# Attention by token tile instead of by head, with the output projection, norm and router of one tile between the attention items of the next

## The reference

```
h = rmsnorm(x);  z = h @ w_in                       # q, k, v and a short gated convolution
s = q.k * scale + bias[bucket];  p = softmax(s)     # 8 maps of 64, in 4 pairs ("heads")
a = p[map 0] - lam * p[map 1];   o = a @ v          # one attention item = one head, 128 queries
o = rmsnorm(o) * 0.8
x = x + concat([o, conv]) @ w_out                   # output projection
h2 = rmsnorm(x);  logits = h2 @ w_router            # one group of 4, 2 of its 4 experts
x = x + sum over chosen experts of gate * (silu(h2 Wg) * (h2 Wu)) Wd
x = x + sigmoid(x @ w_ple_gate) * rmsnorm(p @ w_ple)
```

## Time and profile before

| | |
|---|---|
| median of 3 runs | 717.28 us (713.4 to 717.65) |
| the profiled execution | 716.85 us, span 715.0 us |
| PE busy | 640.3 us, 90% |
| DVE / ACT / POOL busy | 402.9 / 331.8 / 91.1 us |
| transfers | 111 MB, mean 155 GB/s |
| TensorE clock granted, mean | 0.957 |

### The profile page before, as it was taken

How to read it: one execution, slowest core, us unless ns; L and a number is a source line. 1 busy time by engine, 2 the same in 40 slices (tenths; PEclk the granted TensorE clock), 3 DMA queues, 4 the chain that set the end, 5 groups by cost and what they waited for, 6 DMA issues and landing times.

```text
span 715.0 us, 8295 instructions
## 1 busy us (share of the span) xinstructions
PE 640.3 (90%) x3026; PEld 511.9 (72%) x3026; DVE 402.9 (56%) x675; ACT 331.8 (46%) x606; POOL 91.1 (13%) x100
## 2 busy tenths in 40 slices
PE   3999999999999779989999895699999999549997
PEld 2786888888887545578788783477877778338885
DVE  4721356443533377745323285669999997735562
ACT  4632222321332478873222376557788876602121
POOL 0000000000000112200000008413244431100000
PEclk9999999999999999999999796789999999859999
DMA  9404215121000411020415437489999998252321
GB/s 321 187 0 149 89 30 169 30 88 30 30 0 1 170 52 52 1 90 9 173 62 195 144 146 300 143 292 338 391 392 402 397 385 327 81 197 89 110 96 59
DMA packets 33352, 111.16 MB, mean 155 GB/s; under 512 B 5112, under 2 KB 5496, under 8 KB 33312
## 3 DMA queue, kind: packets, MB, share of 16 engines
q1 hardware_dynamic: 27744, 97.39, 37.6%
q0 software_dynamic: 4752, 12.59, 4.5%
q10 hardware_dynamic: 816, 0.66, 0.4%
HBM read 100.62 MB, written 14.71 MB: 161 GB/s over the span
## 4 chain that ended last, share of the span: by engine, by line
PE 72%; DVE 12%; DMA 8%; ACT 3%; issue 3%; SPq 1%; POOL 1%; POOLq 0%; DVEq 0%; ACTq 0%
PE bank L434 21%; PE bank L436 20%; PE bank L435 20%; PE bank L1491 6%; DMA moe_x<-h_rows,slot_token 4%; DVE w_split L413 3%; DVE s L1080 2%; DMA w_raw<-in_w_in 2%; PE bank L1650 1%; PE bank L1520 1%; DVE s L1095 1%; PE bank L1499 1%; DVE moe_xT L1360 1%; DMA w_raw<-in_w_out 1%; PE bank L1537 1%
## 5 line engine op out<-in xcount | busy, mean ns | idle before, releaser
L434 PE MATMUL bank<-w_split,h_T 128*128 128x512 f32 x288 | 116.5, 404 | 0.0
L436 PE MATMUL bank<-w_split,h_T 128*128 128x512 f32 x288 | 113.0, 392 | 0.0
L435 PE MATMUL bank<-w_split,h_T 128*128 128x512 f32 x288 | 112.7, 391 | 0.0
L429 DVE TENSOR_TENSOR w_split<-w_raw,w_split 128x1024 fp32r<-128x1024 f32 x34 | 41.5, 1223 | 45.3 <-ACT w_split L424 45.2
L434 PEld LDWEIGHTS bank<-w_split,h_T 128*128 128x128 f32 x288 | 54.6, 190 | 11.7 <-issue 1.3
L436 PEld LDWEIGHTS bank<-w_split,h_T 128*128 128x128 f32 x288 | 54.3, 189 | 11.8
L435 PEld LDWEIGHTS bank<-w_split,h_T 128*128 128x128 f32 x288 | 54.6, 190 | 11.0 <-issue 0.5
L434 PE MATMUL bank<-w_split,moe_xT 128*128 128x512 f32 x128 | 54.6, 427 | 7.0 <-DVE moe_xT L1360 6.5
L413 DVE TENSOR_TENSOR w_split<-w_raw,w_split 128x1024 fp32r<-128x1024 f32 x48 | 56.7, 1221 | 4.3 <-ACT w_split L407 4.0
L413 DVE TENSOR_TENSOR w_split<-w_raw_more,w_split 128x1024 fp32r<-128x1024 f32 x44 | 52.0, 1220 | 5.7 <-ACT w_split L407 5.7
L436 PE MATMUL bank<-w_split,moe_xT 128*128 128x512 f32 x128 | 51.9, 406 | 0.0
(11 more groups left out here) (220 smaller groups left out, 1243.7 us busy)
## 6 DMA issues: line engine op xcount, KB each, us to landing
w_raw<-in_w_moe SPq DMA_DIRECT2D x54, 512.0 KB, 7.1
w_raw_more<-in_w_moe SPq DMA_DIRECT2D x42, 512.0 KB, 7.8
w_raw<-in_w_in SPq DMA_DIRECT2D x24, 512.0 KB, 6.5
pick<-moe_rows SPq DMA_DIRECT2D x12, 512.0 KB, 4.5
w_raw<-in_w_out SPq DMA_DIRECT2D x8, 512.0 KB, 4.6
toep<-bias_table SPq DMA_DIRECT2D x4, 896.0 KB, 4.7
x_tile<-in_x SPq DMA_DIRECT2D x6, 512.0 KB, 11.9
x_again<-in_x SPq DMA_DIRECT2D x6, 512.0 KB, 3.3
```

Source lines behind the costliest of these rows:

```text
L429: nc.vector.tensor_tensor(W[:, u % WS, 1], raw(u)[0], f(W[:, u % WS, 0]), ALU.subtract).then_inc(lo_done, 1)
L434: nc.tensor.matmul(out, hi, whi, start=first, stop=False)
L435: nc.tensor.matmul(out, lo, whi, start=False, stop=False)
L436: return nc.tensor.matmul(out, hi, wlo, start=False, stop=last)
```

## The change

`ITEMS` is now ordered by tile, but for the first eight, which mix tiles 0 and 1. From the third tile on four items are one tile. When a tile's four items are done, its output goes through the norm, `turn_o`, the projection, x2, `turn_h2` and the router in pieces, and the pieces stand between the items of the next tile. A half of a tile's projection for one half of K (12 matmuls) is cut into two chunks of 6, one before turn_a(w-1), one behind. For this:

- PE runs scores(w), chunk, turn_a(w-1), chunk, pv(w-1); bank 7 is shared by turn_a, turn_o, turn_h2 and the router.
- The four bias tables lie in memory of their own, all loaded right after the input projection, ahead of the late units of w_out.
- The inverse root is no longer Sqrt and DVE's reciprocal, but Ln and then Exp(-0.5 x) on ACT, once a tile for the outputs (`o_std`), once a tile for x2 (`x2_stats`), and once for the last norm.
- The late splits stand at w = 1 to 4, ahead of exps and evac_aT.
- x is loaded again through one buffer in the weight ring, the h2 tiles lie there too; the first expert's six units are loaded after the last router instead of before it.

```diff
-        ITEMS = [(h, i) for h in range(HEADS) for i in range(TILES)]
+        ITEMS = [(0, 0), (0, 1), (1, 0), (2, 0), (3, 0), (1, 1), (2, 1), (3, 1)] + [
+            (h, i) for i in range(2, TILES) for h in range(HEADS)]
-        LATE_UNITS = {2 + j: OUT0 + 4 + j for j in range(4)}
+        LATE_UNITS = {1 + j: OUT0 + 4 + j for j in range(4)}
+        LAST_ITEM = [max(w for w in range(NI) if ITEMS[w][1] == i) for i in range(TILES)]
+        O_AT = {LAST_ITEM[i] + 2: i for i in range(TILES)}
+        CONV_AT = {**{2: (0, 0), 4: (0, 1)},
+                   **{9 + 4 * i + half: (i + 1, half) for i in range(4) for half in range(2)}}
+        ATT_AT = {7 + 4 * i + half: (i, half) for i in range(TILES - 1) for half in range(2)}
+        STAT_AT = {9 + 4 * i: i for i in range(4)}
+        H2_AT = {10 + 4 * i: i for i in range(4)}
+        SPLIT_AT = {7 + 4 * i: i + 1 for i in range(5)}
...
@@ SP @@
-            toeplitz(1)
+            sp.wait_ge(pe_acc, 36)
+            for h in range(1, HEADS):
+                toeplitz(h)
             for u in range(OUT0 + 4, PLE0):
                 unit(w_out[u - OUT0], u)
-            toeplitz(2)
-            toeplitz(3)
...
+            sp.wait_ge(d_x2, 2 * TILES)
+            sp.wait_ge(pe_r, TILES)
+            for j in range(2, 4):
+                unit(w_moe[0, j], MOE0 + j)
+            store_h2(TILES - 1)
+            for half in range(2):
+                sp.wait_ge(h_st[half], 16 * TILES // 2)
+            sp.wait_ge(pe_h2, 2 * TILES)
+            for j in (0, 1, 4, 5):
+                unit(w_moe[0, j], MOE0 + j)
...
@@ ACT @@
+            def o_std(i):
+                ss = o_ssq[:, HEADS * i:HEADS * (i + 1)]
+                act.wait_ge(a_o, 2 * (LAST_ITEM[i] + 1))
+                act.activation(ss, ss, ACT.Ln, bias=eps[:], scale=1.0 / VD).then_inc(a_os, 1)
+                act.wait_ge(a_os, 2 * i + 1)
+                act.activation(ss, ss, ACT.Exp, scale=-0.5).then_inc(a_os, 1)
...
+            split_conv_hi(0)
             exps(1)
-            for w in range(2, NI + 3):
-                if w < NI + 2:
-                    evac_aT(w - 2)
-                if w < NI:
-                    exps(w)
...
+            for w in range(1, NI + 1):
+                if w - 1 in O_AT:
+                    mix_hi(O_AT[w - 1])
+                for half in range(2):
+                    if w - 1 - half in H2_AT:
+                        h2T_out(H2_AT[w - 1 - half], half)
+                if w >= 2:
+                    o_out(w - 2)
+                if w in O_AT:
+                    o_std(O_AT[w])
                 if w in LATE_UNITS:
                     slot_free(act, LATE_UNITS[w])
                     split_hi(LATE_UNITS[w])
+                if 2 <= w < NI:
+                    exps(w)
+                evac_aT(w - 1)
+                if w in SPLIT_AT:
+                    split_conv_hi(SPLIT_AT[w])
+                if w in STAT_AT:
+                    x2_stats(STAT_AT[w])
+            o_out(NI - 1)
+            o_std(TILES - 1)
+            x2_stats(TILES - 2)
+            mix_hi(TILES - 1)
...
@@ DVE @@
+            split_conv_lo(0)
+            for w in range(1, NI + 1):
+                if w - 1 in O_AT:
+                    mix_lo(O_AT[w - 1])
+                if w - 3 in H2_AT:
+                    logits(H2_AT[w - 3])
+                if 2 <= w < NI:
                     scores(w)
                 if w in LATE_UNITS:
                     split_lo(LATE_UNITS[w])
+                if w - 1 in ATT_AT:
+                    x2_sum(*ATT_AT[w - 1])
+                if w in O_AT:
+                    o_norm(O_AT[w])
+                if w in H2_AT:
+                    h2_norm(H2_AT[w])
+                if w in SPLIT_AT:
+                    split_conv_lo(SPLIT_AT[w])
+                if w < NI:
+                    combine(w)
...
@@ PE @@
+            for w in range(1, NI + 1):
+                if 2 <= w < NI:
                     scores(w)
+                chunk(w, 0)
+                if w - 1 in O_AT:
+                    pe.wait_ge(d_mix, O_AT[w - 1] + 1)
+                for half in range(2):
+                    if w - 1 - half in H2_AT:
+                        pe.wait_ge(a_h2, 2 * H2_AT[w - 1 - half] + half + 1)
+                if w - 3 in H2_AT:
+                    pe.wait_ge(d_r, H2_AT[w - 3] + 1)
+                turn_a(w - 1)
+                chunk(w, 1)
+                pv(w - 1)
+                if w in O_AT:
+                    turn_o(O_AT[w])
+                for half in range(2):
+                    if w - half in H2_AT:
+                        turn_h2(H2_AT[w - half], half)
+                if w - 2 in H2_AT:
+                    router(H2_AT[w - 2])
+            conv_part(TILES - 1, 0)
+            pe.wait_ge(d_r, TILES - 2)
+            turn_o(TILES - 1)
+            conv_part(TILES - 1, 1)
+            for half in range(2):
+                turn_h2(TILES - 2, half, 3 + half)
+            att_part(TILES - 1, 0)
+            pe.wait_ge(a_o, 2 * NI)
+            router(TILES - 2, 0)
+            att_part(TILES - 1, 1)
```

More of the change, by code:

```diff
@@ new lines, in _ @@
+            x_again(0)
+            for u in range(PLE0, MOE0):
+                unit(w_ple[u - PLE0], u)
+            for i in range(1, TILES):
+                x_again(i)
+                if i < TILES - 1:
+                    store_h2(i - 1)
+            sp.wait_ge(pe_o, NI)
+            sp.dma_start(p_raw[:], pT).then_inc(p_ld, 16)
+            sp.dma_start(gain[:], gains[2]).then_inc(gain_ld, 16)
+            sp.dma_start(cl[:], late).then_inc(late_ld, 16)
+            store_h2(TILES - 2)
@@ L769, in _ @@
                         if i == 0:
-                            table(ACT.Exp, 1)
+                            table(ACT.Ln, 1)
+                            for m in range(TJ[GATE_B] + 2, TJ[GATE_B] + TILES):
+                                t_ready(act, m)
                         act.wait_ge(pe_acc, n + 1)
@@ L1205, in x2_sum, with h2_norm @@
+            def h2_norm(i):
+                if i == 0:
+                    dve.wait_ge(gain2_ld, 16)
+                dve.wait_ge(a_x2, 3 * i + 3)
                 for half in range(2):
                     c = slice(half * N, (half + 1) * N)
[L1207 to L1219 removed]
@@ L1237, in _ @@
+            logits(TILES - 3)
+            o_norm(TILES - 1)
+            x2_sum(TILES - 2, 1)
+            mix_lo(TILES - 1)
+            h2_norm(TILES - 2)
+            for u in range(PLE0, MOE0):
+                split_lo(u)
+            for half in range(2):
+                x2_sum(TILES - 1, half)
+            logits(TILES - 2, 0)
+            h2_norm(TILES - 1)
             dve.wait_ge(a_p, 1)
@@ L1317, in _ @@
             dve.wait_ge(late_ld, 16)
-            dve.wait_ge(h_st, 16 * TILES)
+            for half in range(2):
+                dve.wait_ge(h_st[half], 16 * TILES // 2)
             link(dve.tensor_tensor(ge_sl[:], bc(r_sl[:].unsqueeze(2), [n2, MOE_TILES + 1]),
@@ L1616, in _, with turn_o, turn_h2, router @@
                                   start=True, stop=True).then_inc(pe_b, 1)
+            def turn_o(i):
+                pe.wait_ge(d_on, i + 1)
+                turn_back(bank[7], o_tok[i % 3], pe_ot)
+            def turn_h2(i, half, b=7):
+                pe.wait_ge(d_h2, 2 * i + half + 1)
+                turn(bank[b], h2[i % 2], 4, pe_h2, 4 * half)
+            def router(i, b=7):
+                pe.wait_ge(a_h2, 2 * i + 2)
+                for k in range(KD):
+                    ins = pe.matmul(bank[b][:, 0:ROUTES], h2T[:, k], wr[:, k],
+                                    start=(k == 0), stop=(k == KD - 1))
+                ins.then_inc(pe_r, 1)
```

404 lines of the change are left out of this document (161 added, 243 removed).

## The result

The changed kernel takes **745.03 us** (median of 4 runs, 741.99 to 746.53); the kernel before, on the same chip, 717.46 us. The ratio is 1.0387, 95% interval 1.0341 to 1.0432: slower by 3.9%. The profiled execution took 745.96 us, its span is 744.1 us, its mean granted clock 0.945 (0.957 before). PE is busy 643.7 us (640.3 before), DVE 404.1 (402.9), ACT 366.2 (331.8), POOL 88.0 (91.1). So only ACT has noticeably more work, and of the 29 us more of span 26 are, on PE, idle time.

What follows compares the result with a forecast made beforehand. Attention was taken as a PE, DVE, ACT loop with PE nearly full. 12.6 + 41.9 + 110.0 + 31.0 = 195.5 us against 172.3, plus 3 for the clock: 716.85 + 26 = 743 us, range 721 to 762.

Steps and rivals of the forecast that it cites:

- The whole: Whole kernel: 716.85 us before plus 26 gives 743 us; the forecast's own case, 726 to 757, had chance 0.68.
- Iteration 1: First item iteration after PE's start: late w_out unit lands at 248.7, then split, copy and pv; 12.6 us.
- The other condition that the prediction named: Iteration 1: ACT's split of the late unit stands ahead of item 0's copy, for which pv(0) waits; split 1.06 us.
- Iterations 2 to 8: Next seven iterations: 5.93 us each with projection pieces, 5.1 for 3 and 5, 8.0 for 6; sum 41.9 us.
- the 3 us for the clock: Iteration 2 and tail: PE's idling brings the 1.2 GHz clock again; bounds nothing and 9 us, 3 taken.
- The inverse root: ACT's Ln and Exp: a table load of 1.28 us ahead of each, 24 more than before, without a drain.
- The rival of one table: Inverse roots on ACT: Ln and Exp share one table, no loads between; about 22 us less, 721 us; chance 0.10.
- The rival with a drain: ACT's table switches: 2.66 us each with drain, or clock staying at 1.2 GHz; 758 to 768 us; chance 0.14.
- The cycles: Four cycles of four iterations from iteration 9: PE waits for ACT's copy and mix_lo; 30.2, 29.3, 25.7, 24.8, sum 110.0 us.
- The tail: From the loop's end to the logits: 3.5 us of idle PE, then last x2, h2, ple_proj(1), router in series; 31.0 us.
- Behind the logits: Logits to first expert: late expert weights hidden by DVE's chain, costed at nothing, up to 2 us if they land late.
- The faster rival: PE's start to logits: overlap works from the start, late units at 244.2, ACT never last; 162 us, 707 in all; chance 0.08.

Runs made afterwards that it cites:

- run 3: The changed kernel with SP issuing the four late w_out units before the wait for V and the three head tables: 734.77 us.
- run 5: The changed kernel with ACT's split of a late weight unit moved back behind the copy of a_T, DVE's half unmoved: 742.75 us.
- run 4: The changed kernel with DVE's split of p_T moved from behind the last tile's h2 norm to between the halves of its x2_sum: 737.8 us.
- run 10: The changed kernel with PE's first two embedding projections put behind the last router, nothing moved on DVE, ACT or SP: 736.77 us.
- run 6: The changed kernel with the last h2 store and the first expert's units 0 and 1 issued before the last router: 741.98 us.
- run 9: The changed kernel with late units first, earlier p_T split, expert units 0 and 1 first, roots on DVE, last router and slot table ahead of projections: 711.04 us.

## Why the prediction was right, point by point

**The whole** (743, measured 745.03) was right in its size and cause: PE's line waits for ACT and for late weights. That it came within 2 us was luck: two of its terms were off by 9 and 7 us and cancelled.

**Iteration 1** (12.6, measured 12.8): right, and run 3 shows the cause, the late issue of the unit on SP's queue. Part of the exact fit is chance: the unit came half a us sooner than reckoned, and pv took 1 us longer at half pace. The other condition that the prediction named, ACT's split ahead of the copy, decided only where the wait fell when it alone was undone (run 5).

**Iterations 2 to 8** (41.9 and some of the 3 us for the clock, measured 43.9): right within 2 us. The granted clock was 0.53 from 245 to 256 us, so the lower level did come, in iteration 1 and at the start of 2.

**The inverse root** (a load at each of Ln and Exp, 1.29 us each, no drain): right. The rival of one table would have been worth 22 us; taking the loads away was worth 17.7 us between the marks, so the rival's price was nearly right and only its condition did not hold. The rival with a drain fell with the rows of iteration 9.

**The cycles** (110.0, measured 100.8): the term was mis-sized. The first cycle was near (30.2, measured 29.4). The step that failed is "With half keys ACT's two chains are as long, but PE's work is shorter: waits of 1.7, 2.3 and 0.4": ACT's chain was started with PE's scores, as in iteration 9, but the router between pv and the scores lets it start 1.5 us ahead of them, and no wait for a_T was left in cycles 3 and 4. The same holds for cycle 2, where 3.0 us of waits were carried over from cycle 1 and 0.6 came. The mechanism holds, at a smaller size: without loads the four cycles lose 7.4 us.

**The tail** (31.0, where its own pieces add up to 30.5; measured 38.3): the term was mis-sized. The step that failed is "x2_sum 0.9, x2_stats 4.2, h2 and transposes 1.9 lie in series, then ple_proj(1)": ple_proj(0) stands ahead of the transposes on PE, its split of p_T behind h on DVE. The order of the change had both rows; I had priced the operation and not its place in the two lines. Runs 4 and 10 show it, 6 us each.

**Behind the logits** (0, up to 2 for late weights; measured 2.5): the size was in sight and the reason was half of it. Besides the late weights, two projections moved ahead of the router left PE idle behind the logits and then slow. Taking away either alone gave at most 0.5 us (runs 6 and 10), and how the 2.5 us divide stays open.

**The faster rival** (707, from a first iteration of 8.1 and ACT never last) needed more than the change had: the late units first, the roots off ACT and PE's tail in another order. With all of these run 9 reaches 711.04; its stretch from PE's start to the logits is 168 us where the rival had 162, mostly in iterations 2 to 8 (40.9 against 33.7), where PE still waits for a_T.

Left open: which part of the 3.1 us of run 6 and of the last 1 to 3 us in other medians is scatter ahead of PE's start; whether both halves of the late split in a later iteration would have hidden the late unit; and why the rest behind the expert's start varies between 271.6 and 276.6 us in the traces.

## What to carry to other kernels

When work is interleaved by hand into one line per engine, write for each wait what stands behind it on that engine, and do this at the seams, too: two of the losses here were an operation in the wrong place (a weight unit behind the tables on the queue, a split behind a norm), and each was mended by moving it, not by making it faster. Moving a waiting instruction back by a few places in one engine's line does little if the instruction that takes its result stands at the old place in another's, or if the operations that it now stands ahead of are needed just as soon; starting the transfer earlier helped. And moving an operation out of the way can gain almost nothing: without the 2.8 us projection ahead of it the router started 1.8 us sooner, ran at half pace and ended 0.1 us sooner.

## What the runs showed of the hardware

- Ln and Exp in turn cost a table load of 1.28 us at every switch, 24 times up to the logits, with nothing behind it: the next operation started 1.29 us after the load's start.
- Nine dependent operations of DVE on 128x4 elements took 1.78 us, 0.2 us each. As an inverse root that is cheaper than Ln and Exp with their two loads (3.0 us) and leaves ACT free.
- The granted clock fell to 0.50, its lower level of 1.2 GHz, around pauses of PE of 6.8 to 10.3 us (iteration 1, and the routing chain in run 6), and to a mean of 0.53 in run 9, where the longest pause shortly before was 1.93 us; the same 16 router matmuls then took 3.58 us instead of 1.85.
